# A two-layer trunk with routed experts: each expert's 3 MB of weights loaded as six transfers of 512 KB in 2 KB pieces instead of three of 1 MB in 8 KB pieces

## What is computed

```python
def hier_moe(h, w_rg, b_rg, w_re, b_re, w_gate, w_up, w_down):
    ...
    # w_gate, w_up: (32, 1024, 256); w_down: (32, 256, 1024) for each layer
    # token-expert pairs are sorted by expert into padded blocks of 128 rows
    def run_block(args):
        xb, e = args
        hid = jax.nn.silu(xb @ w_gate[e]) * (xb @ w_up[e])
        return hid @ w_down[e]
    out = lax.map(run_block, (buf.reshape(nblk, MOE_BLOCK, D), blk_e)).reshape(R, D)
    y = jax.ops.segment_sum(out[dest] * sw[:, None].astype(out.dtype), stok, num_segments=T)
```

## Time and profile before

| | us |
|---|---|
| median of 3 runs (lowest, highest) | 3112.49 (3107.74, 3113.11) |
| the profiled execution | 3107.11 |
| its span | 3105.4 |
| PE busy / its weight loads | 2649.3 / 2227.5 |
| DVE busy | 1788.5 |
| ACT busy | 1260.9 |
| POOL busy | 630.7 |
| mean DMA rate | 164 GB/s |

### The profile page before, as it was taken

One profiled execution on the slowest core, in us unless ns is written; L12 is line 12 of the kernel. 1 busy time (PEld: TensorE's weight loads), 2 busy tenths in 40 slices (PEclk: granted clock), 3 DMA queues, 4 the chain that ended last, 5 costly groups with the idle time before them and its releaser, 6 DMA issues. The chain is left out here.

```text
span 3105.4 us, 48676 instructions
## 1 busy us (share of the span) xinstructions
PE 2649.3 (85%) x15111; PEld 2227.5 (72%) x15112; DVE 1788.5 (58%) x3189; ACT 1260.9 (41%) x2370; POOL 630.7 (20%) x836
## 2 busy tenths in 40 slices
PE   5999979997968947999997699699869957989987
PEld 4999958875847846777775587578758846777776
DVE  4222246665755665668664577588733355686664
ACT  3222132225841104557653322188711104675553
POOL 1000023321110002222222233211100002433333
PEclk9999989998988978999998799899979968999999
DMA  6111112215536515668764455432154414898895
GB/s 237 51 56 54 39 60 78 75 65 165 162 124 229 201 61 192 230 265 314 310 240 167 146 182 171 143 122 86 58 194 141 144 52 151 284 369 254 262 302 123
DMA packets 182222, 509.09 MB, mean 164 GB/s; under 512 B 60760, under 2 KB 88416, under 8 KB 157152
## 3 DMA queue, kind: packets, MB, share of 16 engines
q1 hardware_dynamic: 149248, 418.33, 37.0%
q0 software_dynamic: 32864, 89.37, 10.3%
HBM read 391.34 MB, written 141.43 MB: 172 GB/s over the span
## 5 line engine op out<-in xcount | busy, mean ns | idle before, releaser
L1650 PE MATMUL ps<-moe_parts,moe_xT 128*128 128x512 f32 x2232 | 539.7, 398 | 12.0 <-issue 11.4
L1650 PEld LDWEIGHTS ps<-moe_parts,moe_xT 128*128 128x128 f32 x2232 | 416.9, 190 | 100.6 <-issue 13.9
L1779 DVE TENSOR_TENSOR moe_parts<-expert_w,moe_parts 128x1024 fp32r<-128x1024 f32 x384 | 450.8, 1220 | 50.7 <-ACT moe_parts L1722 35.3
L1148 PE MATMUL ps<-out_w,out_catT 128*128 128x512 f32 x1344 | 321.0, 398 | 14.2 <-DVE out_w L1304 11.8
L582 PE MATMUL ps<-in_gate_w,in_gate_hnT 128*128 128x384 f32 (+1 forms) x1536 | 318.1, 366 | 7.4 <-DVE in_gate_w L716 7.4
L1722 ACT ACTIVATE moe_parts<-expert_w 128x1024 fp32r<-128x1024 f32 x256 | 261.8, 1049 | 111.0 <-PEq L155 79.0
L582 PEld LDWEIGHTS ps<-in_gate_w,in_gate_hnT 128*128 128x128 f32 x1536 | 277.4, 189 | 37.5 <-issue 7.5
L1148 PEld LDWEIGHTS ps<-out_w,out_catT 128*128 128x128 f32 x1344 | 254.6, 191 | 69.1 <-DVE out_w L1304 12.6
L1650 PE MATMUL ps<-moe_parts,moe_hidT 128*128 128x512 f32 x1116 | 287.3, 407 | 2.5 <-ACT moe_y L1743 2.5
L582 PE MATMUL ps<-in_qk_w,in_qk_hnT 128*128 128x512 f32 x1152 | 267.8, 393 | 9.2 <-DVE in_qk_w L716 9.2
L582 PEld LDWEIGHTS ps<-in_qk_w,in_qk_hnT 128*128 128x128 f32 x1152 | 216.6, 189 | 54.3 <-issue 9.5
(11 more groups left out here) (270 smaller groups left out, 4110.6 us busy)
## 6 DMA issues: line engine op xcount, KB each, us to landing
expert_w<-in_w_gate SPq DMA_DIRECT2D x64, 1024.0 KB, 9.3
expert_w<-in_w_up SPq DMA_DIRECT2D x64, 1024.0 KB, 11.2
expert_w<-in_w_down SPq DMA_DIRECT2D x64, 1024.0 KB, 6.9
hn_d<-out_hn SPq DMA_DIRECT2D x32, 512.0 KB, 2.6
out_w<-y_d SPq DMA_DIRECT2D x32, 512.0 KB, 6.1
in_gate_xt<-in_x SPq DMA_DIRECT2D x16, 512.0 KB, 3.5
in_qk_xt<-in_x SPq DMA_DIRECT2D x16, 512.0 KB, 3.5
att_k<-k_d SPq DMA_DIRECT2D x64, 128.0 KB, 2.9
```

Of the source, the lines that this page charges most:

```text
L1148: last = nc.tensor.matmul(yp[:, 512 * half:512 * (half + 1)], catT[:, s.slot(2), a, k, :], w[:, b, k, 512 * half:512 * (half + 1)], start= ...
L1650: last = nc.tensor.matmul(out, left[:, a, k, :], right(b, k), start=(a + b + k == 0), stop=(a == 1 and k == K_ - 1))
L1779: nc.vector.tensor_tensor(parts[:, j, 1, at], K.expert_w[:, j, at], parts[:, j, 0, at].bitcast(F32), ALU.subtract).then_inc(done, 1)
```

## The change

Each of the three transfers of an expert becomes two of 512 KB. Within a slot the gate and up weights now lie by pairs of rows: for each of four pairs q, first the two rows of gate (512 floats, 2 KB), then the two rows of up. So the first half of the place, which is free after two split pieces, takes the first two pairs of both gate and up, and the second half the other two. The down weights lie by halves of 512 columns, the two rows of a partition side by side within a half. The number of floats, the places of the pieces that ACT and DVE split, and the points at which SP waits are as before; the semaphores count 64 and 32 where they counted 32 and 16. In memory a piece of gate or up weights is now 2 KB on the side of the chip and 4 KB in a row on the side of the memory, and a piece of down weights 2 KB in memory and 4 KB in a row on chip. PE's right-hand operand of `raise_` is read as two runs of 256 floats that lie 512 floats apart, where they lay 2048 apart.

```diff
 def load_up(K, sp, layer, e, slot, until_free=lambda n: None):
 
-    for n, name in enumerate(("w_gate", "w_up")):
+    place = K.expert_w[:, slot, 0:DK * 2 * FF].rearrange("p (q s c) -> p q s c", q=DK // 2, s=2)
+    for n in range(2):
         until_free(n)
-        src = K.x[name][layer].rearrange("e (p k) f -> e p (k f)", k=DK)
-        src = src[e] if isinstance(e, int) else src[bass.ds(e, 1)].rearrange("a p f -> (a p) f")
-        sp.dma_start(K.expert_w[:, slot, n * DK * FF:(n + 1) * DK * FF], src).then_inc(K.up_in[layer][slot], 16)
+        for s, name in enumerate(("w_gate", "w_up")):
+            src = K.x[name][layer].rearrange("e (p q t) f -> e p q (t f)", q=DK // 2, t=2)
+            src = src[e] if isinstance(e, int) else src[bass.ds(e, 1)].rearrange("a p q c -> (a p) q c")
+            at = slice(n * DK // 4, (n + 1) * DK // 4)
+            sp.dma_start(place[:, at, s, :], src[:, at, :]).then_inc(K.up_in[layer][slot], 16)
 
 def load_down(K, sp, layer, e, slot):
 
-    src = K.x["w_down"][layer].rearrange("e (p k) n -> e p (k n)", k=2)
-    src = src[e] if isinstance(e, int) else src[bass.ds(e, 1)].rearrange("a p n -> (a p) n")
-    sp.dma_start(K.expert_w[:, slot, DK * 2 * FF:], src).then_inc(K.down_in[layer][slot], 16)
+    place = K.expert_w[:, slot, DK * 2 * FF:].rearrange("p (h k c) -> p h k c", h=2, k=2)
+    src = K.x["w_down"][layer].rearrange("e (p k) n -> e p k n", k=2)
+    src = src[e] if isinstance(e, int) else src[bass.ds(e, 1)].rearrange("a p k n -> (a p) k n")
+    for h in range(2):
+        sp.dma_start(place[:, h, :, :], src[:, :, 512 * h:512 * (h + 1)]).then_inc(K.down_in[layer][slot], 16)
...
-                wgu = parts[:, j, :, 0:GU].rearrange("p h (s k f) -> p h k s f", s=2, k=DK)
+                wgu = parts[:, j, :, 0:GU].rearrange("p h (q s t f) -> p h q t s f", q=DK // 2, s=2, t=2)
...
-                product(gup, xT, lambda h, k: wgu[:, h, k, :, :], DK, ((0, 0), (0, 1)))
+                product(gup, xT, lambda h, k: wgu[:, h, k // 2, k % 2, :, :], DK, ((0, 0), (0, 1)))
...
-                wd = parts[:, j, :, GU:EW].rearrange("p h (k n) -> p h k n", k=2)
+                wd = parts[:, j, :, GU:EW].rearrange("p h (e k n) -> p h e k n", e=2, k=2)
...
-                                       lambda h, k: wd[:, h, k, 512 * half:512 * (half + 1)], 2, terms)
+                                       lambda h, k: wd[:, h, half, k, :], 2, terms)
...
-                a.wait_ge(K.down_in[layer][j], i * 16 + 16)
+                a.wait_ge(K.down_in[layer][j], i * 32 + 32)
...
-                    a.wait_ge(K.up_in[layer][nj], ni * 32 + 32)
+                    a.wait_ge(K.up_in[layer][nj], ni * 64 + 64)
```

More of the change, by code:

```diff
@@ L1661, in raise_ @@
             def raise_(m, j):
-                wgu = parts[:, j, :, 0:GU].rearrange("p h (s k f) -> p h k s f", s=2, k=DK)
+                wgu = parts[:, j, :, 0:GU].rearrange("p h (q s t f) -> p h q t s f", q=DK // 2, s=2, t=2)
                 until(pe, x_high, m + 1)
                 until(pe, hid_done, m)
-                product(gup, xT, lambda h, k: wgu[:, h, k, :, :], DK, ((0, 0), (0, 1)))
+                product(gup, xT, lambda h, k: wgu[:, h, k // 2, k % 2, :, :], DK, ((0, 0), (0, 1)))
                 until(pe, x_low, m + 1)
-                product(gup, xT, lambda h, k: wgu[:, h, k, :, :], DK, ((1, 0),)).then_inc(up.sem, 1)
+                product(gup, xT, lambda h, k: wgu[:, h, k // 2, k % 2, :, :], DK, ((1, 0),)).then_inc(up.sem, 1)
             def turn_hid(m):
@@ L1764, in block_ @@
                 y_scaled(m - 2)
-            a.wait_ge(K.up_in[layer][0], 32)
+            a.wait_ge(K.up_in[layer][0], 64)
             split_up(0, range(GU_PIECES))
```

## The result

The changed kernel takes 3156.24 us (median of 4 runs, 3148.42 to 3158.8), the kernel before beside it 3111.23 (4 runs). The ratio is 1.0133, 95% interval 1.0109 to 1.0156: about 41 us slower, where the forecast was 24 faster and the range ended at 3124. The profiled execution took 3156.07 us, its span is 3154.4.

What follows compares the result with a forecast made beforehand. The prediction took PE's waits for gathered rows, and second the DMA itself, as the bound. Its terms 11.7 - 17.6 - 19.4 - 3 + 3.5 = -24.8 gave 3088 us against the median, range 3062 to 3124.

Steps and rivals of the forecast that it cites:

- The gather beside small pieces, -17.6 and -19.4: Experts: gathers land 1.8 us sooner beside 2 KB pieces, cutting PE's waits by 17.6 us in layer 0, 19.4 in layer 1.
- Turns of eight: Rival on the DMA queues: engines send eight weight pieces, then eight gather rows; 1.1 us saved a gather, 3097 us, chance 0.15.
- Pieces of 2 KB, +11.7: Weights' queue: smaller pieces cost 12% more engine time, 0.9 us an expert, exposed on 13 experts of layer 1.
- More transfers, nothing: Weights' loads: three more transfers an expert cost nothing, since transfers' ends were passed at a DMA share of 100.3%.
- The saturated stretches, 0.9 a block: Layer 1 where the DMA has no room: each block lengthens by 0.9 us, to 12 us in place of 11.1.
- Layer 0 from 1400 to 1540, nothing: Single-block experts there: nothing counted, as PE would wait for weights instead of rows; bounds 10.7 us gained or 5 lost.
- the sign of being wrong: The prediction is wrong if ACT's waits for weights grow beyond its slack of 2.5 us in layer 0 also.
- Clock, -3: Both layers: with PE's stands some of the lowered clock after them goes too, 3 us gained, bounds 0 and -8.
- PE, ACT, DVE, nothing: The new layout on chip, read at another stride, costs these engines nothing; bounds -2 and +2 us.
- More issues on SP, nothing: Three more issues an expert, 0.33 us each, end about 1 us later but hide behind queued transfers: nothing.
- The first 6 MB, +3.5: First two experts' weights, issued within the output projection: 1.8 us more in each layer, all exposed, 3.5 us lost.
- The slower rival: Rival: pieces cost engine time and the gather gains nothing, since engines share time or bytes; +26, 3138 us, chance 0.18.

Runs made afterwards that it cites:

- e8: Kernel before with gate and up still whole transfers, but in 2 KB pieces and both issued behind the second wait of `load_up`; down as before: 3094.5 us.
- e9: Kernel before with gate and up whole in 8 KB pieces, both issued behind the second wait of `load_up`; down as before: 3128.6 us.
- e16: Changed kernel with each of its six transfers an unbroken 512 KB of memory, same 2 KB pieces and order of issue: 3112.6 us, ratio 0.9994.
- e14: Kernel before with gate and up in the change's four transfers of 2 KB pieces, each an unbroken 512 KB of memory; down as before: 3096.8 us.
- e15: As e14, with down also in two unbroken transfers of 512 KB, in 4 KB pieces: 3103.9 us, ratio 0.9966.
- e13: Kernel before with seven added stages of 4 MB loads, whole or halved, skipping or unbroken, each alone in layer 0's `route`: 12.8 to 15.9 us a stage.
- e10: Changed kernel with all four transfers of gate and up issued behind the second wait of `load_up`: 3147.0 us, ratio 1.0102.
- e3: Kernel before with only the down weights changed, to two transfers by column halves in 2 KB pieces: 3177.4 us, ratio 1.0211.

## Why the prediction was wrong, point by point

- **What bounds the kernel.** Right: the gather's landing and, in layer 1, the DMA. The first is borne out by e8 and e9, in which the pieces of gate and up alone turn 100.4 us of gather waits into 43.1; the second by the stands before `raise_` in layer 1.
- **The gather beside small pieces, -17.6 and -19.4.** The direction is right and the size not far off: 2 KB pieces of gate and up are worth 43 us, and in e16 the waits are 32.6 below the kernel before. In the change itself they did not fall (83.3 to 84.3; in layer 0 they grew), so the landings below 7.5 us did not come where halved transfers skip. The reason given, that the engines serve the queues piece for piece, is wrong: 1.4 to 1.6 packets of weights go to one of the gather, and time is shared about evenly (44.9% and 49.3%). Turns of eight would have left the counts level too. That rival drew on the Trainium skill, page "DMA: Bandwidth & Descriptors", section "Queues, rings and completion order", by which an engine drains a packet of about 9 to 17 descriptors from one ring before the next. The traces do not tell the engines apart, so no run here shows how long a turn is.
- **Pieces of 2 KB, +11.7.** 0.9 us an expert was forecast. e16 has 1.0 more than before, so the pieces were priced about right; the change has 1.4 in the quiet part, and 1.1 (7.6 to 8.7) where the DMA is full.
- **More transfers, nothing.** This is the step that failed. It took halving as a matter of transfers' ends, and its lower and upper bound were both nothing. The row it used (937 to 944, share 100.3%) is of whole transfers, which pass over nothing. The change's section says that a piece of gate is 4 KB in a row in memory and a piece of down 2 KB; what lies between them is passed over by each transfer, and no term priced that. Measured: 43 us (the change against e16). Of the number itself e8 to e14 (7 us, the order changed too) and e14 to e15 (5 us) show little, and neither is clear of the noise. The Trainium skill, page "DMA: Bandwidth & Descriptors", asks in its section "Bandwidth" for at least 1 MiB a transfer, and the direction agrees. The fixed 2 us or so of its section on the anatomy of a DMA, as 6 us an expert, would be far too much: 4 MB in eight unbroken transfers of 4 KB pieces took 13.25 us in e13, in four whole ones 12.83.
- **The saturated stretches, 0.9 a block.** This step failed too, by its size: a saturated block takes 13.6 us and not 12. Beyond ACT's slack, 2.6 us in the earlier trace rows and 2.1 in the block shown above, each microsecond that the up weights are late is one of PE's. Even in e16, which skips nothing, the stands before `raise_` are 21.8 us above the kernel before, and with the slower matmuls they take back what the gather gains: it ends 2 us below the kernel before, not 25.
- **Layer 0 from 1400 to 1540, nothing.** About right for the gather (10.7 us of waits, now 12.4), but the sign of being wrong that the prediction named came true: in layer 0 also ACT waits beyond its slack, 6.7 us at the longest.
- **Clock, -3.** Wrong in sign: the stands grew, and the matmuls of `raise_` took 11.5 us more; behind the stand of 7.25 us they are 1.4 times as long. Layer 1's stretch is at 0.92.
- **PE, ACT, DVE, nothing.** Right: 84 of 93 blocks' `raise_` take about 5.75 us, as before.
- **More issues on SP, nothing.** Each issue was taken to last 0.33 us. It lasts 0.4 to 2.2 us here, and the last one of the weights waited for above is 4.1 us behind down (2.2 in the kernel before). e10 and the change differ by 9 us, not clear of the noise, so the place of the issues is the smaller part.
- **The first 6 MB, +3.5.** +1.0 in layer 0 (12.8 to 13.8) and +0.4 in layer 1 (3.6 to 4.0): 1.4 in all.
- **The slower rival** came nearest, at 3138. Its outcome for the gather came true in the change (waits of 83.3 and 84.3 us), but not for its reason, that the engines share time or bytes: e8 shows that small pieces do help the gather.

## What to carry to other kernels

Before a load is cut in two, ask what each half leaves out in memory, not only how large its pieces are: here the same six transfers cost 43 us more when each skipped every other 2 or 4 KB than when each was one unbroken stretch (how much of down's share is its 2 KB runs in memory is not parted), and a change of which rows go to which partition is enough to make them so. Small pieces on a bulk queue can be worth having for a latency-bound gather beside it (43 us here), if the bulk transfers stay whole or unbroken; here the late landing of the weights themselves then took most of it back in the halved loads. And read GB/s beside the DMA share: a full share at 308 GB/s is not the full share at 406.

## What was not expected of the hardware

- Transfers to 64 partitions move 225 GB/s with the engines at a share of 0.99, those to 128 partitions 408: the cost is hidden in the packets' time and looks like a full engine.
- Alone on the queue, halved transfers that skip memory start slowly (252 to 261 GB/s over 4 to 6 us) and reach 403 later, while halves that skip nothing (320) and a 1 MB transfer that skips (357) start faster. Which part of the path makes the two together slow is open.
- SP's issue of a transfer takes 0.33 us for 8 KB pieces, 0.38 to 0.65 for 2 KB pieces, and up to 2.18 us while many are in flight (2738.83).
- How long PE stood does not tell whether its clock falls. In e3 a stand of 2.79 us was followed by a granted clock of 0.62 over 3.9 us, and 12 matmuls took 4.58 us in place of 3.01. In the kernel before, a stand of 2.79 us at 1621.91 was followed by full clock, one of 1.92 at 1259.13 too, but those of 1.81 at 2878.95 and of 1.92 at 3019.03 by clocks of 0.66 and 0.64 and 4.58 us.
